# Second MLP projections: two of three products in one 512-column matmul, and two residual updates per tile

## The reference, cut to what matters

```python
h = rms_norm(x, mlp_norm_g[i]) * (1.0 + sc2) + sh2
x = x + g2 * (jnp.square(jax.nn.relu(h @ mlp_w1[i])) @ mlp_w2[i])
```

## Time and profile before

| | us |
|---|---|
| median of 3 runs | 1424.93 (1423.87 to 1427.14) |
| profiled execution, span from first to last instruction | 1423.9 |
| PE busy | 1328.9 |
| DVE busy | 947.5 |
| ACT busy | 586.0 |

### The profile page before, as it was taken

One profiled execution on the slowest core, in us unless ns is written; L12 is line 12 of the kernel. 1 busy time (PEld: TensorE's weight loads), 2 busy tenths in 40 slices (PEclk: granted clock), 3 DMA queues, 4 the chain that ended last, 5 costly groups with the idle time before them and its releaser, 6 DMA issues.

```text
span 1423.9 us, 20770 instructions
## 1 busy us (share of the span) xinstructions
PE 1328.9 (93%) x8774; PEld 1206.3 (85%) x8774; DVE 947.5 (67%) x1381; ACT 586.0 (41%) x863; POOL 0.2 (0%) x4
## 2 busy tenths in 40 slices
PE   2989789999989989899999999999999998997996
PEld 2988779999989857899999999888888887985776
DVE  6799886767776564678676763774846745647754
ACT  4436456455344343454544422321213213624643
POOL 0000000000000000000000000000000000000000
PEclk8899999999999956999999999999999999996999
DMA  9542367667757500376664452432433422330000
GB/s 367 210 158 92 149 233 270 255 258 284 265 201 302 205 32 1 123 270 242 220 254 165 167 189 90 159 112 88 176 145 118 148 90 81 121 117 0 1 1 30
DMA packets 32380, 227.41 MB, mean 160 GB/s; under 512 B 3600, under 2 KB 3856, under 8 KB 5152
## 3 DMA queue, kind: packets, MB, share of 16 engines
q1 hardware_dynamic: 32288, 226.09, 43.3%
HBM read 225.03 MB, written 1.05 MB: 159 GB/s over the span
## 4 chain that ended last, share of the span: by engine, by line
PE 82%; DVE 10%; ACT 4%; issue 3%; DMA 1%; SPq 0%; ACTq 0%; DVEq 0%
PE prod L1343 22%; PE prod L1345 21%; PE prod L1344 21%; PE prod L1549 4%; PE misc L1310 3%; DVE acc L788 3%; PE prod L1528 2%; DVE w_lo L765 2%; PE prod L1499 2%; ACT w_hi L472 2%; PE misc L1318 2%; PE misc L1445 1%; DMA raw<-stream 1%; PE prod L1474 1%; DVE rows L859 1%
## 5 line engine op out<-in xcount | busy, mean ns | idle before, releaser
L765 DVE TENSOR_TENSOR w_lo<-raw,w_hi 128x2048 fp32r<-128x2048 f32 x138 | 316.2, 2291 | 329.6 <-ACT w_hi L472 329.6
L472 ACT ACTIVATE w_hi<-raw 128x2048 fp32r<-128x2048 f32 x138 | 264.1, 1914 | 552.9 <-PE prod L1345 546.6
L1343 PE MATMUL prod<-XH,w_hi 128*128 128x256 f32 (+1 forms) x1360 | 426.9, 314 | 35.7 <-DVE XL L874 22.7
L1344 PE MATMUL prod<-XL,w_hi 128*128 128x256 f32 (+1 forms) x1360 | 421.4, 310 | 0.0
L1345 PE MATMUL prod<-XH,w_lo 128*128 128x256 f32 (+1 forms) x1360 | 421.0, 310 | 0.0
L1343 PEld LDWEIGHTS prod<-XH,w_hi 128*128 128x128 f32 x1360 | 267.5, 197 | 51.0 <-issue 34.7
L1344 PEld LDWEIGHTS prod<-XL,w_hi 128*128 128x128 f32 x1360 | 267.7, 197 | 11.2 <-issue 0.7
L1345 PEld LDWEIGHTS prod<-XH,w_lo 128*128 128x128 f32 x1360 | 267.4, 197 | 11.0
L788 DVE SCALAR_TENSOR_TENSOR acc<-raw,cond,acc 128x1024 f32<-128x1024 f32 x168 | 210.0, 1280 | 5.5 <-DMA raw<-stream 2.7
L1343 PE MATMUL prod<-FH,w_hi 128*128 128x256 f32 (+1 forms) x640 | 197.2, 308 | 1.1 <-DVE w_lo L765 1.1
L1345 PE MATMUL prod<-FH,w_lo 128*128 128x256 f32 (+1 forms) x640 | 196.1, 306 | 0.0
(11 more groups left out here) (201 smaller groups left out, 1389.4 us busy)
## 6 DMA issues: line engine op xcount, KB each, us to landing
raw<-stream SPq DMA_DIRECT2D x210, 1024.0 KB, 4.9
X<-x_features SPq DMA_DIRECT2D x1, 1024.0 KB, 11.3
C<-ctx_features SPq DMA_DIRECT2D x1, 1024.0 KB, 8.3
out_features<-HT SPq DMA_DIRECT2D x4, 256.0 KB, 2.4
WS<-spatial_w SPq DMA_DIRECT2D x1, 512.0 KB, 5.7
BS<-spatial_b SPq DMA_DIRECT2D x1, 512.0 KB, 6.5
SM<-constants SPq DMA_DIRECT2D x1, 512.0 KB, 5.8
col<-params SPq DMA_DIRECT2D x1, 289.0 KB, 3.1
```

Of the source, the lines that this page charges most:

```text
L472: A(w_hi[:, w % SPLITS, :, :].rearrange("p k c -> p (k c)"), raw[:, n % RING, :], ACT.Copy).then_inc(weight_hi, 1)
L765: tt(w_lo[:, w % SPLITS, :, :].rearrange("p k c -> p (k c)"), raw[:, n % RING, :], w_hi[:, w % SPLITS, :, :].rearrange("p k c -> p (k c)") ...
L1343: mm(out, lhs_hi, rhs_hi, start=start, stop=False)
L1344: mm(out, lhs_hi, rhs_lo, start=False, stop=False)
```

## The change

The high and low parts of the hidden activations of one quarter are laid side by side, per k: [high 256 | low 256]. High weights times both are one matmul of 512 columns, whose two column blocks go to the two halves of the PSUM bank; low weights times high activations add to the first half in a matmul of 256 columns. The drain adds both halves to X in two updates of 256 columns, the second waiting for the first; the counts of `x_updated` follow.

```diff
-UPDATES = {"conv_out": 2, "w2": 2, "wo": 2, "a_out": 4, "b_out": 2}
+UPDATES = {"conv_out": 2, "w2": 4, "wo": 2, "a_out": 4, "b_out": 2}
...
+        FF = [f[:, :].rearrange("p (k s t) -> p k s t", k=KT, s=2) for f in (FH, FL)]
...
-                    squares(n, X, H, lambda k: act.wait_ge(x_updated, LAST_XU[n] + k + 1),
+                    squares(n, X, H, lambda k: act.wait_ge(x_updated, LAST_XU[n] + PER_TILE[n] * (k + 1)),
...
-                    dve.wait_ge(x_updated, max(1, count["x"] - 7))
+                    dve.wait_ge(x_updated, max(1, count["x"] - 6))
...
-                    fl = F_lo[:, u[2] % 2, 2 * u[3]:2 * u[3] + 2, :]
+                    fl = FF[u[2] % 2][:, 2 * u[3]:2 * u[3] + 2, 1, :]
...
-                        update_x(lambda: stt(out=X[:, k, :], in0=tiles(w, T)[:, i, :],
-                                                   scalar=g, in1=X[:, k, :], op0=ALU.mult,
-                                                   op1=ALU.add))
+                        for half in range(2 if kind == "w2" else 1):
+                            if half:
+                                dve.wait_ge(x_updated, count["x"])
+                            update_x(lambda: stt(out=X[:, k, :],
+                                                 in0=tiles(w, 2 * T)[:, i, T * half:T * (half + 1)],
+                                                 scalar=g, in1=X[:, k, :], op0=ALU.mult,
+                                                 op1=ALU.add))
...
+                        if kind == "w2":
+                            mm(tiles(w, nt)[:, i, :], wh[:, k, P * i:P * (i + 1)], both[:, k, :, :],
+                               start=(k == 0), stop=(k == KT - 1), skip_group_check=True)
+                            ins = mm(tiles(w, nt)[:, i, 0:T], wl[:, k, P * i:P * (i + 1)],
+                                     both[:, k, 0, :], start=False, stop=(k == KT - 1),
+                                     skip_group_check=True)
+                            continue
```

More of the change, by code:

```diff
@@ L160 @@
 XU_MLP0 = XU_CONV + 8
-XU_WO = XU_MLP0 + 32
+XU_WO = XU_MLP0 + 64
 XU_MLP1 = XU_WO + 8
-XU_A = XU_MLP1 + 32
+XU_A = XU_MLP1 + 64
 XU_B = XU_A + 32
@@ L182 @@
 STAT_DONE = [1, 3, 4, 5, 6, 9, 10, 12]
-LAST_XU = {2: XU_CONV, 3: XU_MLP0 + 24, 4: XU_WO}
+LAST_XU = {2: XU_CONV, 3: XU_MLP0 + 48, 4: XU_WO}
+PER_TILE = {2: 1, 3: 2, 4: 1}
 COLS = {}
@@ L324, in build @@
         RSB = EV[:, :, :].rearrange("p a (b c) -> p (a b) c", c=P)
-        F_hi = FH[:, :].rearrange("p (b k t) -> p b k t", b=2, k=KT)
-        F_lo = FL[:, :].rearrange("p (b k t) -> p b k t", b=2, k=KT)
+        FF = [f[:, :].rearrange("p (k s t) -> p k s t", k=KT, s=2) for f in (FH, FL)]
         G_hi = FH[:, :].rearrange("p (k t) -> p k t", k=KT)
@@ L547, in drain @@
                     act.wait_ge(f_sq, f + 1)
-                    A(F_hi[:, u[2] % 2, 2 * u[3]:2 * u[3] + 2, :], ei, ACT.Copy).then_inc(f_hi, 1)
+                    A(FF[u[2] % 2][:, 2 * u[3]:2 * u[3] + 2, 0, :], ei, ACT.Copy).then_inc(f_hi, 1)
                 elif kind in ("q", "k"):
@@ L742, in _ @@
                     j = s - (CTX_AT + 4)
-                    act.wait_ge(x_updated, XU_A - 8 + 2 * (j + 1))
+                    act.wait_ge(x_updated, XU_A - 16 + 4 * (j + 1))
                     modulated_hi(0, X, 0, (2 * j, 2 * j + 1))
@@ L934, in drain @@
                     dve.wait_ge(f_hi, f + 1)
-                    fl = F_lo[:, u[2] % 2, 2 * u[3]:2 * u[3] + 2, :]
-                    fh = F_hi[:, u[2] % 2, 2 * u[3]:2 * u[3] + 2, :]
+                    fl = FF[u[2] % 2][:, 2 * u[3]:2 * u[3] + 2, 1, :]
+                    fh = FF[u[2] % 2][:, 2 * u[3]:2 * u[3] + 2, 0, :]
                     tt(fl, ei, fh.bitcast(F32), ALU.subtract).then_inc(f_lo, 1)
@@ L1281, in _ @@
                     j = s - (CTX_AT + 4)
-                    dve.wait_ge(x_updated, XU_A - 8 + 2 * (j + 1))
+                    dve.wait_ge(x_updated, XU_A - 16 + 4 * (j + 1))
                     dve.wait_ge(unit_done, UNITS.index(("w1", 1, 3, 3)) + 1)
@@ L1380, in unit @@
                         pe.wait_ge(f_lo, 16 * u[1] + 4 * (u[2] + 1))
-                        hi, lo, nt = F_hi[:, u[2] % 2], F_lo[:, u[2] % 2], T
+                        both, nt = FF[u[2] % 2], 2 * T
                     elif kind == "a_out":
```

## The result

The changed kernel took 1432.71 us (median of four runs, 1431.86 to 1435.91) against 1425.32 for the kernel before: 1.0057 times, 95% interval 1.0042 to 1.0072, or +7.4 us. Forecast were 1429.2 and +4.3. So the sign was right, the rise is 1.7 times the forecast one, and the time lies 1.2 us above the forecast's own range (1427 to 1431.5), inside the wider one with the free wait and the dear pair (1424.2 to 1433.2). The profiled execution has a span of 1431.5 against 1423.9. Two executions far above all others, 2167.61 us of the kernel before and 5098.16 of e11_delay, are left out everywhere.

What follows compares the result with a forecast made beforehand. PE was taken to set the pace, with DVE or ACT late in places. Four places, -1.1 + 2.1 + 0.8 + 2.5 = +4.3 us, on the median 1424.93 gave 1429.2 us; own range 1427 to 1431.5, wider 1424.2 to 1433.2.

Steps and rivals of the forecast that it cites:

- the free wait: Rival on the DVE drain: an update waiting for the previous one costs nothing extra; 1426.1 us, chance 0.17.
- the dear pair: Rival: PE's mixed pair of matmuls saves nothing or DVE's waits are dear; 1432.1 us, chance 0.14.
- DVE's price: Second-projection drain on DVE: four updates instead of two, 1.82 us instead of 0.79, +1.03 each.
- PE's price: Second-projection units on PE: matmuls of 512 plus 256 columns take 0.347 instead of 0.360 us, 0.213 saved a unit.
- (d): End of the second MLP: a DVE and ACT loop without PE makes a_v's first unit wait; +2.5 us.
- (a): First MLP, 16 second-projection units: DVE's loop uses up most of PE's gain; -1.1 us.
- (b): Second MLP, first group: longer drains plus modulation chunks delay w_lo and PE; +2.1 us.
- (c): Second MLP, second group: a longer drain and chunk delay w_lo, one unit's gain remains; +0.8 us.
- hidden drains: Rival: DVE's idle time takes all added updates, so PE's full 6.8 us comes; 1418.1 us, chance 0.08.
- One sign of being wrong: Second MLP, first group: forecast wrong if PE's starts at 664.32 and 675.93 move forward.
- the clock: Rival: shifted timing and PE idle add or remove a 1.7 us clock dip; 1427.5 or 1430.9, chance 0.11.
- nothing lies around the span: Whole kernel: profiled span 1423.9 equals the quickest run's 1423.87, so no time lies outside the span.

Runs made afterwards that it cites:

- e11_delay: e2_pe_alone with 14 dummy matmuls (1.7 us) between the first two units of a_v, to move the reduction behind in time: 1425.15 us.
- e1_order: The changed kernel with each drain updating the first column block of both tiles, then the second, so no update waits for the one just before: 1428.11 us.
- e12_again: The changed kernel run once more, unaltered, beside the later experiments: 1432.02 us.
- e8_spread: The changed kernel with six reductions of tiny matmuls spread call by call between the matmuls of the next unit: 1418.88 us.
- e6_spread: The kernel before the change with six reductions of tiny matmuls spread call by call between the matmuls of the next unit: 1417.39 us.
- e4_fill: The changed kernel with dummy matmuls where PE waits for DVE in the second MLP (16, 10, 16 and 30): 1427.96 us.
- e9_tail_out: The changed kernel with the last quarter of the second MLP put back to three matmuls and two updates: 1426.46 us.
- e2_pe_alone: The changed kernel with joined matmuls but only the first column block drained, in two updates as before; high x low product left out: 1424.80 us.
- e5_free: The changed kernel joined only in four quarters where DVE has room, first block of both tiles updated before the second: 1420.50 us.
- e10_only_first: The changed kernel joined only in the whole first MLP and the third quarter of the second: 1421.46 us.

## Why the prediction was right in sign and short in size

**DVE's price** held: 1.82 forecast, 1.83 measured. The rival with the free wait falls by e1_order: its drain of 1.57 is what a free wait would have given, and it took another order to get it. The rival of the dear pair had 1432.1, next to the measured 1432.71, by chance: its pair saves nothing and its waits are dear, and neither is so. The sentence of the Trainium skill ("VectorE: DVE Perf Modes", "The DRAIN you can't avoid") that a semaphore between chained DVE operations costs nothing extra does not agree with 0.51 against 0.40 here; for a wait on the operation before the last it does.

**PE's price** held in some units and not in others. The step of the pair (PE, over 32 matmuls of the first MLP, then over 32 of the second):

```profile
359.26 0.39 PE L1401 MATMUL prod<-FH,w_hi 128*128 128x512 f32 x1
359.49 0.27 PE L1403 MATMUL prod<-FH,w_lo 128*128 128x256 f32 x1
359.60 0.40 PE L1401 MATMUL prod<-FH,w_hi 128*128 128x512 f32 x1
...
364.69 0.28 PE L1403 MATMUL prod<-FH,w_lo 128*128 128x256 f32 x1
...
763.05 0.40 PE L1401 MATMUL prod<-FH,w_hi 128*128 128x512 f32 x1
...
768.59 0.28 PE L1403 MATMUL prod<-FH,w_lo 128*128 128x256 f32 x1
```

359.26 to 364.69 is 5.43 for 31 steps, 0.231 and 0.115 in turn, a pair of 0.346; 763.05 to 768.59 is 5.54, a pair of 0.354. So in (d) the five units brought 0.5 and not 1.0. The MLP does not decide it. The second trace of the change (e12_again) has the units of (d) at the first figure:

```profile
768.78 0.40 PE L1401 MATMUL prod<-FH,w_hi 128*128 128x512 f32 x1
...
774.22 0.27 PE L1403 MATMUL prod<-FH,w_lo 128*128 128x256 f32 x1
```

That is 5.44, and (d) is +2.7 there. Its first MLP has units of 5.54 (315.04 to 320.58), and the second MLP of the change has one of 5.43 (712.81 to 718.24). What decides it is open. The 2.5 ns that the Trainium skill ("TensorE: Matmul & The Clock Gate", "Back-to-back issue gap") gives, for a matmul by itself, would save 2.5 ns of 0.360, a pair of 0.358; the faster units speak for the rows' 0.347, and the slower ones lie nearer to the page's figure.

**The places.** (a) -1.1 was forecast; L857 went from 404.84 to 401.55, of which 2.2 came from before the MLP, -1.1. DVE's loop there, in which w_lo to w_lo is 6.40 (forecast 6.51):

```profile
382.33 1.91 DVE L955 SCALAR_TENSOR_TENSOR X<-prod,mod,X 128x256 f32<-128x256 f32 x4
386.53 2.29 DVE L765 TENSOR_TENSOR w_lo<-raw,w_hi 128x2048 fp32r<-128x2048 f32 x1 [2.29 <-ACT w_hi L472]
...
392.94 2.29 DVE L765 TENSOR_TENSOR w_lo<-raw,w_hi 128x2048 fp32r<-128x2048 f32 x1 [0.32 <-ACT w_hi L472]
...
401.55 0.42 DVE L857 TENSOR_SCALAR rows<-misc 128x256 f32<-128x256 f32 x1
```

(b) +2.1, measured +2.3; (c) +0.8, measured +0.9. (d) +2.5, measured 3.1 and 2.7, by the unit gain above; the loop itself is as worked out (784.25 to 803.22 was 18.97, 784.43 to 806.94 is 22.51, +3.5). Together +5.1 in both traces, +4.1 over nine runs and +4.8 between e8_spread and e6_spread by the subtraction, for 4.3. That PE would not get its 6.8 us, and that hidden drains would not decide, is shown. One sign of being wrong was badly put: PE's starts at 664.32 and 675.93 did move forward, to 659.74 and 672.57, because 5.5 us had been gained ahead of them, 2.2 of it before the change's first unit; held against the unit before the group they come 0.9 and 2.2 later, as forecast.

**The step that failed** is the clock: "Shifted timing, and 2.1 us of idle instead of 0.65 before the unit of 664.32, may add or remove one", a rival at 0.11 and at nothing in the sum. It is a term of +2 to +3 us: 7.2 in the nine runs less the 5.1 of the places or the 4.1 of the subtraction. In the table it is 6.9 from 726 on, less 2.2 and 2.2 ahead of it. The rest of the miss is the places, 5.1 for 4.3. e4_fill shows its place and its sign: with DVE as late as in the change but the waits filled, 4.7 us go. Three traces bear it out: in the change, e12_again and e9_tail_out a dip to 0.77 stands behind the wait of 1.8 to 1.9 us at 726 and its like, while e1_order, with 1.56 us there, has 1.00. The largest single dip, 2.3 us, lies where I did not look at all, in a_v's first unit behind (d). I had forecast its tile 4.3 us late (it came 3.7 late), and did not carry the wait that this makes, 3.75 us, on to the clock.

**What stays open** is what decides a kernel's low-clock time. Idle PE alone does not: e2_pe_alone has 8 us more of it than the kernel before and 0.8 us more waiting, e8_spread 6 less than e6_spread and more waiting, e5_free and e10_only_first 6 to 8 less. Nor does a wait of 1.9 us always bring a dip: the one at 659.74 has none behind it. A part of the difference is which of the six reductions have a dip behind them: five in the traces of the kernel before and of the change, all six in e2_pe_alone, four in e5_free and e4_fill. Why one is spared is open; e11_delay was to tell and did not. A forecast by place could have had +4 to +5 and a few us of clock of unknown sign.

**Beside the sum**, "nothing lies around the span" is wrong: it compared the span of one run with the time of another. Every run's time is 1.9 to 2.1 us above its own span (1433.41 and 1431.5). Both kernels have it, so the difference is not touched.

## What to carry to other kernels

Before moving work from the bounding engine to one at 67%, compare that engine's loop with the unit time stretch by stretch, and make the exchange only where there is room: the same edit in 4 of 8 quarters (with the better order) gained 4.4 us, 3 of them on the path, and in all 8 lost 7. Order dependent updates so that none waits for the one right before it. Don't let PE run tiny matmuls in a row or wait where the path is tight, and put a price on the clock for each new wait.

## What the runs showed of the hardware

- Reductions of 32 one-column matmuls in a row, some 3.5 us each, are mostly followed by a granted clock of 0.84 to 0.90 over the next 11 to 17 us (five of six in the kernel before; the one at 1052.20 has 1.00); call by call among 256-column matmuls they are not, and six of them so placed gained 7.5 us.
- Matmuls whose result nobody uses paid: 72 of them, in PE's waits, took 4.7 us off.
- An update of 128x256 that waits for the one right before it starts 0.51 us behind it, one that waits for the one before that 0.40.
- At the lower clock 256 columns take 0.213 us a step, at the higher 0.120: not twice as long, but 1.78 times.
- Kernels with almost the same work differ by 145 to 180 us in time at the lower clock, up to some 17 us of time, and executions of one of them (e4_fill) by 13 us. A gain of 0.3% is not to be told from one execution.
- A matmul of 512 columns with one of 256 behind it, steps of 0.231 + 0.115 or 0.237 + 0.117, is not the sum of the two alone (0.2266 and 0.120): the short one is cheaper and the long one dearer. Which of the two figures a unit has changes within an execution and between executions of the same kernel.
